# Two phases of row gathers re-cut: all V rows of block 0 in phase 1, and a pace table of its own for that phase

## The reference, cut to what matters

```
h = rms_norm(x);  proj = h @ w_in                  # (1024 x 2816)
x = x + [attention || retention](proj) @ w_out     # (1024 x 1024)
xn = rms_norm(x);  q = xn @ w_q                    # (1024 x 2048), 8 heads x 2 halves x 128
s = q . sub_keys;  sv, si = top_k(s, 16)           # per head and half, 128 keys
top_s, pos = top_k(sv0[i] + sv1[j], 16)            # 16 of 256 pairs
expert = 128 * si0 + si1;  g = softmax(top_s)      # 8 x 16 = 128 experts a token
hid = gelu(u_table[expert] . xn)                   # 128 rows of 1024 floats a token
x = x + sum_k (g * hid)[k] * v_table[expert[k]]    # 128 rows of 1024 floats a token
y = rms_norm(x)
```

## Time and profile before

| | us |
|---|---|
| runs shown, median (3 runs) | 3637.41 |
| lowest and highest | 3636.71, 3653.42 |
| profiled execution, its own time | 3651.41 |
| its span | 3649.3 |

### The profile page before, as it was taken

One profiled execution on the slowest core, in us unless ns is written; L12 is line 12 of the kernel. 1 busy time (PEld: TensorE's weight loads), 2 busy tenths in 40 slices (PEclk: granted clock), 3 DMA queues, 4 the chain that ended last, 5 costly groups with the idle time before them and its releaser, 6 DMA issues. The chain is left out here.

```text
span 3649.3 us, 27702 instructions
## 1 busy us (share of the span) xinstructions
PE 1989.2 (55%) x9448; PEld 1092.7 (30%) x9448; DVE 2038.2 (56%) x4571; ACT 324.0 (9%) x778; POOL 2103.3 (58%) x2183
## 2 busy tenths in 40 slices
PE   6975563766673447657734367557634332223446
PEld 6764441544550115324501034324301000000001
DVE  2379747567648674674565744755675644444120
ACT  2211010111100010111100010101000000000000
POOL 0045523656556675665566765666676766666665
PEclk9986786886885668768956579668756655655669
DMA  6588965999999999999999999999998999999998
GB/s 224 179 302 287 392 234 184 343 397 355 381 383 376 371 368 395 401 368 367 397 394 353 344 378 394 392 370 394 404 349 328 368 376 375 373 364 386 366 362 323
DMA packets 442170, 1286.15 MB, mean 352 GB/s; under 512 B 39408, under 2 KB 157936, under 8 KB 442032
## 3 DMA queue, kind: packets, MB, share of 16 engines
q0 software_dynamic: 313344, 1140.99, 82.0%
q1 hardware_dynamic: 126224, 134.48, 11.0%
q10 hardware_dynamic: 2464, 8.91, 0.6%
HBM read 1274.50 MB, written 9.44 MB: 352 GB/s over the span
## 5 line engine op out<-in xcount | busy, mean ns | idle before, releaser
L926 DVE CUSTOM_DVE_ANT_0 ring<-ring,ps 128x1024 f32<-128x1024 f32 x1088 | 1298.2, 1218 | 929.7 <-DMA ring<-in_peer_u_dram,u_idx 777.6
L658 POOL DMA_INDIRECT ring<-in_peer_u_dram,u_idx x1088 | 1038.6, 955 | 809.4 <-issue 286.4
L1243 PE MATMUL ps<-ring,spread 128*32 128x512 f32 x4352 | 884.2, 916 | 1122.5 <-DMA ring<-in_peer_v_dram,v_idx 1011.2
L658 POOL DMA_INDIRECT ring<-in_peer_v_dram,v_idx x1088 | 1062.9, 977 | 718.6 <-issue 292.9
L1284 PE MATMUL ps<-wbuf,actT 128*128 128x256 f32 (+1 forms) x2944 | 712.0, 401 | 135.4 <-issue 94.9
L1243 PEld LDWEIGHTS ps<-ring,spread 128*32 128x32 f32 x4352 | 180.5, 143 | 1717.8 <-issue 1700.9
L1284 PEld LDWEIGHTS ps<-wbuf,actT 128*128 128x128 f32 (+1 forms) x2944 | 563.0, 195 | 317.5 <-issue 213.6
L999 DVE MAX8 work<-work 128x8 f32<-128x128 f32 (+3 forms) x432 | 109.6, 325 | 84.5 <-ACT work L895 68.0
L1003 DVE FIND_INDEX8 work<-work 128x8 uint32<-128x128 f32 (+3 forms) x432 | 134.3, 335 | 15.6 <-issue 15.6
L728 ACT COPY spread<-weightT 128x16 f32<-128x16 f32 x64 | 14.0, 219 | 924.6 <-PE ps L1243 487.6
L926 DVE DVE_READ_ACCUMULATOR2_ANT hidden<- 128x1 f32 x1088 | 90.2, 83 | 1.1 <-issue 1.1
(11 more groups left out here) (153 smaller groups left out, 1283.8 us busy)
## 6 DMA issues: line engine op xcount, KB each, us to landing
wbuf<-in_w_in_dram SPq DMA_DIRECT2D x55, 1024.0 KB
wbuf<-in_peer_w_q_dram SPq DMA_DIRECT2D x40, 1024.0 KB
wbuf<-in_w_out_dram SPq DMA_DIRECT2D x20, 1024.0 KB
ring<-in_peer_u_dram,u_idx POOLq DMA_INDIRECT x1088
ring<-in_peer_v_dram,v_idx POOLq DMA_INDIRECT x1088
x_v<-x_scratch ACTq DMA_DIRECT2D x8, 512.0 KB
out_dram<-x_v ACTq DMA_DIRECT2D x8, 512.0 KB
x_in<-in_x_prompt_dram SPq DMA_DIRECT2D x7, 512.0 KB
```

What stands on the lines that cost most here:

```text
L658: pool.indirect_dma_start(ring[:, at % RING, :], None, table, bass.IndirectOffsetOnAxis(ap=idx, axis=0)).then_inc(landed[at % RING], 16)
L926: ch.put(v_.tensor_tensor_reduce(out=row, in0=row, in1=ux_ps, scale=1.0, scalar=0.0, op0=ALU.mult, op1=ALU.add, accum_out=hidden[:, k:k + ...
L1243: mm = pe.matmul(ps[j:j + 32, B_ACC + c, :], spread[:, at:at + 32], tile[:, 512 * c:512 * c + 512], start=(t % 32 == 0), stop=(t % 32 == 3 ...
```

## The change

The first half moves V rows 64 to 127 of block 0 from phase 2 to phase 1. The second gives phase 1 (`begun`) widths of its own. The table's numbers are only ratios: an item's place is the step's base over the total, times the items.

```diff
 PHASES = [
     ([0], [], []),
-    ([1, 2], [0], [(0, 0, 64)]),
-    ([3, 4], [1, 2], [(0, 64, 128), (1, 0, 128)]),
+    ([1, 2], [0], [(0, 0, 128)]),
+    ([3, 4], [1, 2], [(1, 0, 128)]),
...
-    NORM, PIECE, ATTN, PEER, BEGUN_PEER = 6, 3.6, 55, 105, 58
+    WIDTH = {"norm1": 6, "w_in": 3.6, "attn": 55, "w_out": 3.6, "norm2": 6, "w_q": 3.6, "peer": 105}
+    BEGUN = {"norm1": 0, "w_in": 1.7, "attn": 24, "w_out": 1.3, "norm2": 2, "w_q": 3.5, "peer": 66}
...
+        self.width = self.BEGUN if begun else self.WIDTH
```

More of the change, by code:

```diff
@@ L228, in __init__ @@
         self.slots = len(items)
+        self.width = self.BEGUN if begun else self.WIDTH
+        self.done = {"w_in": g * EARLY} if begun else {}
+        times = {"w_in": N_IN, "w_out": N_OUT, "w_q": N_Q}
         at, self.base = 0.0, {}
[L230 to L234, removed]
+        for name, width in self.width.items():
             self.base[name] = at
-            at += width
+            at += (g * times.get(name, 1) - self.done.get(name, 0)) * width
         self.total = at
@@ L241, in __init__ @@
             if kind == "load" and u + UXBUF in blocks:
[L242 to L246, removed]
+                self.floors.append((self.base["norm2"] + self.width["norm2"] * blocks.index(u + UXBUF), n + 1))
     def slot(self, step, n, part=0.0):
```

## The result

The changed kernel takes 3683.66 us (median of 4 runs, 3667.48 to 3687.26) where the kernel before took 3638.48 in the same session (4 runs, 3636.71 to 3653.42): a ratio of 1.0106, with a 95% interval of 1.0066 to 1.0147. Forecast were 3592 us and a range of 3550 to 3638. The direction was wrong: 45 us were to be won, and 45 were lost. The profiled execution took 3681.7 us with a span of 3679.5; before it was 3651.4 with 3649.3.

The account below looks back on a forecast made before the run. The prediction took the kernel to be bound by a DMA stream of 2176 row gathers, with time won only where it pauses. Terms 0 + 27 - 72 = -45 us took the median from 3637.4 to 3592 us, range 3550 to 3638.

Parts of the forecast that it names:

- (c): Phase 2, norm to top-k, with 64 V rows fewer: 627 us against 699, -72; bounds -86 and -50.
- rival 4: Slower: unpaced full queue holds up products in phase 1 (+30), block 3's w_in (+29), phase 2's top-k (+26); 3677, chance 0.06.
- (a): Phase 1 up to the top-k at 504: earlier w_q start offset by a longer full queue, 0; bounds -16 and +10.
- the bound of +10: Phase 1's w_q: no more than 5 products pass in the full stretch, ending at 499, plus 5 for a later stall.
- (b): Top-k of phase 1: 114 V rows still to land, block 3's transposes at 671, not 644: +27; bounds +10 and +38.
- The price of 1.42: Phase 1's top-k: us per V row beside nothing else, from 211 gathers in 300 us late in the run.
- The bound of -50: Phase 2's smallest gain: w_in and attention as long as before, the top-k 10 us longer than worked out.
- The rule of the skill: DMA engines alternate between queues with work, a packet at a time, so 1040 weight packets should pass beside 1040 of the gathers.
- Rival 2: Phase 1's w_q: weights pass beside the full gather queue packet for packet, 16 us more gained: -61, 3576, chance 0.07.
- Rivals 1 and 3: First: stream never pauses, -82, 3555, chance 0.14. Second: phase 2 gives gain back, V rows at 1.52, -12, 3625, chance 0.18.
- The sign named for rival 4: In the changed profile, w_in of block 3 at 140 us or more would show the forecast wrong.

Follow-up runs that it names:

- the kernel with steps: Changed kernel, with VectorE's U rows beside w_in and w_q tied to the products, one step each: 3595.4 us against 3640.7 on chip 10, ratio 0.9880.
- The kernel before with steps: Kernel before the change, with VectorE's U rows in w_in and w_q tied to the products: 3624.6 us, ratio 0.9929 on chip 4.
- the new division alone: Kernel before, with only the new division of V rows and the old pace: 3393.9 us, 0.9949 (chip 9); 3663.9 us, 1.0058 (chip 4).

## Why the prediction was wrong, point by point

**The step that failed** is in (c): "the queue is as full as in 401 to 444 and weights come late as in (a): I add 10, 118 (bounds 108 and 125)". w_in took 164. Its mechanism was misnamed, too: not weights came late but the signals of finished products, and on this kind of chip products whose weights lay ready were held up by that. Of the miss of 91 us at the start of phase 3, 47 are here. What would have led to it stood in the prediction. The earlier trace rows show two waits of 19 and 21 us beside unpaced U rows, and its own rival 4 said what follows if VectorE takes 64 of them before attention: 4 products pass beside them, 18 behind, 147 us. Four copies beside and 18 behind (805 to 864, 59 us) is what came. That it was 164 and not 147 is the length of the first part: rival 4 had 64 rows in 85 us, and the 107 us of row five hold 72 (145 records, 1.49 us a row for 1.33). The chance for it was 0.06, on the argument that w_in took 5.7 us a product in phase 2 before. That row was of a stretch with V rows' quads among the products, which the order shows, and which the change took out. So the counter-argument rested on the very interleaving that the change removed.

**(a) right, by luck in part.** 0 predicted, +4 measured. The full stretch was forecast as 80 us from 381 to 461 and was 75 from 376 to 451. It passed 6 products, of which 4 were copied by its end, and not 7 or 8: the bound of +10 had named about that. The waits in it, of 29, 23 and 18 us:

```profile
419.37 0.37 ACT L876 COPY wide<-ps 128x256 f32<-128x256 f32 x1 [29.11 <-remote]
442.59 0.37 ACT L876 COPY wide<-ps 128x256 f32<-128x256 f32 x1 [22.84 <-remote]
460.93 0.65 ACT L876 COPY wide<-ps 128x256 f32<-128x256 f32 x2 [17.97 <-remote]
```

That the cost was there, hidden by the earlier start, the kernel with steps shows: its w_q takes 95 us and ends at 466, the change's on the same chip takes 131 and ends at 505.

**(b) right in kind, too small.** +27 predicted with bounds +10 and +38, +43 measured. (By its own numbers the lower bound is 504 + 114 x 1.31 + 5 = 658, which is +14.) Block 2's top-k began at 601 for 573, not a few us later. TensorE's transposes of block 3 begin at 694.7 and not at 671: (694.7 - 507.8 - 5)/114 = 1.60 us for a V row beside the top-k, above the bound of 1.52. The price of 1.42 was from a stretch at 375 GB/s that has nearly nothing but gathers. The stretches here run at 337 and 331 GB/s, as the 345 of the earlier trace rows warned; the nearest row in kind was that one.

**(c) otherwise.** Attention -11 for -9: right. The top-k of phase 2 -30 for -38: the 26 gathers fewer were worth 1.15 us each and not 1.48. w_out, norm 2 and w_q 0 for -18: wrong by 18. Its copies show three of the same waits:

```profile
1066.14 0.37 ACT L876 COPY wide<-ps 128x256 f32<-128x256 f32 x1 [17.14 <-remote]
1079.57 0.65 ACT L876 COPY wide<-ps 128x256 f32<-128x256 f32 x2 [13.05 <-remote]
...
1127.83 0.65 ACT L876 COPY wide<-ps 128x256 f32<-128x256 f32 x2 [16.48 <-remote]
```

With steps the same stages take 143 us (915 to 1058). The bound of -50 is also off by its own numbers: w_in and attention as before and a top-k 10 longer make 653 us, which is -46.

**The rule of the skill.** Rival 2 rested on a turn between queues by packets (The Trainium skill, DMA: Bandwidth & Descriptors, Queues, rings and completion order). No run here shows it, and it did not matter: the piece of 762 to 783 passed in 20 us too, and the products waited for something else. The rows do not refute it either: the page's packet is typically 9 to 17 descriptors, and whether the packets that the earlier trace rows count are such packets or single descriptors, nothing here shows.

**Rivals 1 and 3** did not come. Attention did not grow, and VectorE was not the bound in phase 2. Of rival 3 only its dear V rows came (1.60 us for its 1.52). **Rival 4** came in its main part, w_in of block 3, and nearly in its time, 3677 for 3684; this is luck in part. Its loss in phase 1 was +4 and not +30, its top-k of phase 2 was 227 and not 252, and (b) and w_out to w_q, which it did not name, took their place. The sign named for rival 4, w_in of block 3 at 140 or more, is the one that the trace shows.

**Shown and not shown.** Shown: without steps for VectorE the change loses 1.1 to 1.2% on the chips of the first kind, with them it gains 1.2%, and the difference falls where the late signals stood; VectorE's reading is not the cause, and the widths of the pace are at most half of it. Not clear: what the change is worth beside steps. The kernel before with steps is at 0.9929 (0.9904 to 0.9955) and the change with steps at 0.9880 (0.9827 to 0.9933), on different chips, and the intervals overlap. Only argued: that the late signals are the whole of the loss. Open: what delays TensorE's signals, why pacing shortens the delay at the same total load, and why it occurs on some chips only. The change itself was not timed on a chip of the other kind; with its parts at -0.5% and +0.5% there, about no change would be my guess.

## What to carry to other kernels

When a change takes an interleaved order apart (here V rows and their quads out from between the products), a stall seen once in a stretch that is already without interleaving is the nearest price for the new stretch, for each product that falls into it; a row from the interleaved stretch is no evidence against it. Give an engine that consumes a prefetch stream a step for every stage of its neighbours, even where it has no work of its own in that stage: that was worth 87 us here on chips of the first kind, and nothing on the other. And time on more than one chip before a pace is chosen by 0.5%: the new division alone won 0.5% on one kind and lost 0.6% on the other.

## What was not expected of the hardware

- **Signals of TensorE that come late.** On the chips of the first kind, up to 1400 us, 42 updates of TensorE's semaphores in the changed kernel came more than 3 us after the end of the last matmul before them that raised one, the longest 25 us; before it was 53, with 16 as the longest. Paired in order, as above, the longest of w_in is 52 us. In the traces of chips 9, 7 and 14 there was none in that time. VectorE's were at most 6 us late, ScalarE's never.
- **Updates that merge.** Of TensorE's 780 signals, 722 updates are recorded in the changed kernel on the first chip and 799, a reset for each semaphore included, on chip 9. A pairing is safe only where both counts agree. Of the landings of DMAs it is 18237 against 37592.
- **Two kinds of chip, 7% apart.** The same kernel takes 3410 us on chips 9, 7 and 14 and 3640 on the first kind. Late in the run the gathers move 409 GB/s on the faster kind and about 375 on the first, as the page of the new division alone shows for chip 9:

```profile
GB/s 241 169 331 355 353 361 385 356 394 345 352 369 404 385 374 394 401 409 401 397 397 390 395 397 394 405 409 398 401 406 395 388 410 409 409 410 410 409 410 337
```

  Between 3100 and 3300 us half of the 4 KB packets take at most 0.16 us on both kinds, but the slowest hundredth takes over 0.5 to 0.6 us on the first kind and over 0.17 on the faster one.
  The Trainium skill (HBM Reference, Specifications (TRN2)) says that two cores share a domain of HBM, and that a core gets less once the other streams too. Whether another core was at work beside this one on the chips of the first kind, no run here shows; it would be one way to a lower rate, and the page says nothing of signals.
